# First conditioning part in two halves of output channels, and the last expert pair in a loop of its own

## What is computed

```python
def adaln_layer(x, mod, lp, s0_f, s0_b, ctx_ckv, ctx_krope):
    sh1, sc1, gt1, sh2, sc2, gt2 = jnp.split(mod, 6, axis=-1)
    h = rmsnorm(x, lp['g_norm1']) * (1 + sc1) + sh1
    mix, s_f, s_b, ckv_n, krope = token_mixers(h, lp, s0_f, s0_b, ctx_ckv, ctx_krope)
    x = x + gt1 * mix
    h = rmsnorm(x, lp['g_norm2']) * (1 + sc2) + sh2
    x = x + gt2 * moe(h, lp)
```

## Time and profile before

| | |
|---|---|
| median of three runs | 856.54 us (855.97 to 858.58) |
| the profiled execution's own time | 856.37 us |
| its span | 854.5 us |
| TensorE busy | 809.0 us, 95% |
| VectorE busy | 396.8 us, 46% |
| ScalarE busy | 140.5 us, 16% |
| moved from and to memory | 257.62 MB, mean 301 GB/s |

### The profile page before, as it was taken

The page is one execution under the profiler, slowest core; times in us unless marked ns, Lnnn a source line. Parts: engine busy times, 40 slices in busy tenths (PEclk is TensorE's granted clock), DMA queues, the critical chain, the costliest instruction groups (busy, mean ns, idle before and its releaser), DMA issues.

```text
span 854.5 us, 14663 instructions
## 1 busy us (share of the span) xinstructions
PE 809.0 (95%) x5589; PEld 423.0 (49%) x5589; DVE 396.8 (46%) x841; ACT 140.5 (16%) x289; POOL 8.3 (1%) x16
## 2 busy tenths in 40 slices
PE   3699999879999999999999999999999999999993
PEld 0355434556545645535545455355454554553552
DVE  1206485573787434443443344334434433443346
ACT  2122110210232201111111111111111111111110
POOL 0000001000000000000000000000000000000000
PEclk9799999989999999999999999999999999999998
DMA  9975445424402999989989989899899899898905
GB/s 352 396 289 185 177 147 197 197 74 163 182 26 69 424 368 366 402 349 387 381 350 395 376 345 419 349 375 392 354 384 379 350 402 371 344 420 352 375 0 196
DMA packets 41780, 257.62 MB, mean 301 GB/s; under 512 B 4572, under 2 KB 7004, under 8 KB 13472
## 3 DMA queue, kind: packets, MB, share of 16 engines
q1 hardware_dynamic: 41760, 257.35, 75.8%
HBM read 253.81 MB, written 3.52 MB: 301 GB/s over the span
## 4 chain that ended last, share of the span: by engine, by line
PE 87%; DVE 7%; DMA 3%; ACT 1%; issue 1%; SPq 0%; DVEq 0%; ACTq 0%
PE ps L508 85%; DMA ada<-in_w_ada 3%; PE ps L948 1%; DVE h L1529 0%; DVE h L1530 0%; DVE x1b L1764 0%; DVE acc L1763 0%; ACT sq L1112 0%; DVE probT L1436 0%; PE ps L783 0%; DVE x L1519 0%; DVE xtmp L1517 0%; DVE attn L1425 0%; DVE keyT L1403 0%; SPq L381 0%
## 5 line engine op out<-in xcount | busy, mean ns | idle before, releaser
L508 PE MATMUL ps<-raw_gu,xs 128*32 128x512 f32 x2048 | 225.6, 592 | 0.0
L508 PEld LDWEIGHTS ps<-raw_gu,xs 128*32 128x32 f32 x2048 | 66.5, 110 | 152.6 <-issue 152.6
L1733 DVE TENSOR_TENSOR acc<-acc,ps 128x512 f32<-128x512 f32 x198 | 120.9, 679 | 0.8 <-PE ps L508 0.8
L508 PE MATMUL ps<-raw_dn,ast 128*32 128x512 f32 x1024 | 116.5, 595 | 0.0
L508 PE MATMUL ps<-ys,place 128*128 128x512 f32 x396 | 107.9, 409 | 1.4 <-DVE ys L1726 1.4
L508 PE MATMUL ps<-pick,h2h 128*128 128x256 f32 x408 | 98.6, 283 | 0.9 <-issue 0.9
L508 PE MATMUL ps<-pick,h2l 128*128 128x256 f32 x408 | 98.6, 283 | 0.0
L1718 DVE SCALAR_TENSOR_TENSOR act_a<-ps,small,sil 128x256 f32<-128x256 f32 x32 | 15.5, 484 | 176.9 <-ACT sil L1174 176.9
L508 PEld LDWEIGHTS ps<-ys,place 128*128 128x128 f32 x396 | 69.6, 189 | 41.1 <-issue 26.8
L508 PEld LDWEIGHTS ps<-pick,h2h 128*128 128x128 f32 x408 | 78.2, 192 | 2.3 <-issue 1.7
L508 PEld LDWEIGHTS ps<-pick,h2l 128*128 128x128 f32 x408 | 78.2, 192 | 0.6
(11 more groups left out here) (283 smaller groups left out, 632.7 us busy)
## 6 DMA issues: line engine op xcount, KB each, us to landing
raw_gu<-in_w_exp_gate SPq DMA_DIRECT2D x64, 1024.0 KB, 8.5
raw_gu<-in_w_exp_up SPq DMA_DIRECT2D x64, 1024.0 KB, 10.8
raw_dn<-in_w_exp_down SPq DMA_DIRECT2D x64, 1024.0 KB, 8.1
ada<-in_w_ada SPq DMA_DIRECT2D x8, 1024.0 KB, 10.2
ada2a<-in_w_ada SPq DMA_DIRECT2D x8, 1024.0 KB, 4.6
ada2b<-in_w_ada SPq DMA_DIRECT2D x8, 1024.0 KB, 4.7
w_out<-in_w_out SPq DMA_DIRECT2D x1, 4096.0 KB, 13.0
w_qk<-in_w_in SPq DMA_DIRECT2D x1, 2048.0 KB, 19.6
```

The costliest lines, as they stand in the source:

```text
L508: return nc.tensor.matmul(out, l, r, start=first, stop=last)
L1733: V.tensor_tensor(a, a, ps[:, 4 + (6 * half + k) % 4, :], ALU.add).then_inc(S["acc_done"], 1)
```

## The change

The first third of `w_ada` is fetched in two passes of eight transfers of 512 KB, pass h with the output columns h * 512 to h * 512 + 511 of shift and of scale (two runs of 2 KB per partition). Each chunk has its own buffer; the second pass of chunk c waits for the first pass's products of that chunk. `hT`'s chunks are now rows c * 128 + p of the model width, so that the first half of the output columns completes chunks 0 to 3; `w_in` is read in that order, and `w_mla` and `w_qk` in two halves by chunk. TensorE runs the first pass, turns it, turns `x_sb`, and puts the second pass's products between the first halves of the `mla` products. The constants `tconst`, `rows` and `wgk` are issued later. In the expert part the last pair has its own loop on TensorE, ScalarE and VectorE, without gather, gate columns, `tokens` and `picks`; the number of pairs before it is a second number in `jobs`.

The diff, cut to its core:

```diff
@@ -377,22 +377,27 @@
-            for c in range(4):
-                sp.dma_start(ada1[:, c, :], w_ada[:, c, 0:2 * D]).then_inc(ada1_in[c], 16)
+            w_in = A["w_in"][0].rearrange("(c p) n -> p c n", p=P)
+            low, high = slice(0, NC // 2), slice(NC // 2, NC)
+            for h in range(2):
+                for c in range(NC):
+                    if h:
+                        sp.wait_ge(S["ada1_used"], c + 1)
+                    cols_ = w_ada[:, c, 0:2 * D].rearrange("p (j n) -> p j n", j=2)[:, :, h * 512:(h + 1) * 512]
+                    sp.dma_start(ada1[:, c], cols_).then_inc(ada1_in[c], 16)
+                if not h:
+                    load(w_mla[:, low], w_in[:, low, 1536:1984], "w_mla_in")
+            load(w_qk[:, low], w_in[:, low, 0:512], "w_qk_in")
+            load(w_mla[:, high], w_in[:, high, 1536:1984], "w_mla2_in")
+            load(w_qk[:, high], w_in[:, high, 0:512], "w_qk2_in")
             load(tconst[:], A["c_trunk"], "consts_in")
             load(rows[:], A["c_rows"].partition_broadcast(P), "consts_in")
             load(wgk[:], A["c_wgk"], "consts_in")
-            w_in = rows_pc(A["w_in"][0], 1984)
-            for c in range(4, NC):
-                sp.wait_ge(S["ada1_used"], c - 3)
-                sp.dma_start(ada1[:, c - 4, :], w_ada[:, c, 0:2 * D]).then_inc(ada1_in[c - 4], 16)
-            load(w_mla[:], w_in[:, :, 1536:1984], "w_mla_in")
-            load(w_qk[:], w_in[:, :, 0:512], "w_qk_in")
             load(krope[:, 3, :], A["cache_mla_krope"][0, 0], "cache_in")
             load(ckvn[:, 3, :], A["cache_mla_ckv"][0, 0], "cache_in")
             load(w_v[:], w_in[:, :, 512:1024], "w_v_in")
             load(w_g[:], w_in[:, :, 1024:1536], "w_g_in")
-            sp.wait_ge(S["ada1_used"], NC)
+            sp.wait_ge(S["ada1_used"], 2 * NC)
@@ -539,58 +544,83 @@
-            for c in range(NC):
-                if c == 4:
-                    pe.wait_ge(S["consts_in"], 16)
-                    pe.wait_ge(S["xn_ready"], 1)
-                    for k in range(NC):
-                        if k >= 4:
-                            pe.wait_ge(S["xT_sb"], k - 3)
-                        for t in range(NT):
-                            last = nc.tensor.transpose(ps[:, 4 + k % 4, t * P:(t + 1) * P],
-                                                       x_sb[:, t, k::NC], ident)
-                        last.then_inc(S["xT_done"], 1)
-                pe.wait_ge(ada1_in[c % 4], 16 * (c // 4 + 1))
-                for n in range(4):
-                    last = mm(ps[32 * n:32 * n + 2, 0, :], silu_c[:, c, :], ada1[:, c % 4, n * 512:(n + 1) * 512], c == 0, c == NC - 1)
+
+            def ada1_piece(h, c):
+                pe.wait_ge(ada1_in[c], 16 * (h + 1))
+                for j in range(2):
+                    for q in range(2):
+                        r = 32 * (2 * j + q)
+                        last = mm(ps[r:r + 2, 4 * h, 0:256], silu_c[:, c, :], ada1[:, c, j, q * 256:(q + 1) * 256], c == 0, c == NC - 1)
                 last.then_inc(S["ada1_used"], 1)
...
+            def mod_t(h):
+                pe.wait_ge(S["mod1_sb"], h + 1)
+                if h:
+                    pe.wait_ge(S["xT_sb"], NC)
+                for k in range(4):
+                    rows_ = ident[0:98, 32 * (k // 2):32 * (k // 2) + 66].rearrange("p (j s) -> p j s", s=2)[:, 0::32, :]
+                    last = mm(ps[:, 5, 16 * h + 4 * k:16 * h + 4 * k + 4], mod1[0:98, h, k % 2 * P:(k % 2 + 1) * P], rows_, True, True)
+                last.then_inc(S["modT_done"], 1)
+
+            def token_rows(n, t, w, cs=range(NC)):
+                o = (open_proj(n) if cs[0] == 0 else pbank(n))[:, 0:w.shape[2]]
+                for c in cs:
                     if n == "mla0":
                         pe.wait_ge(S["h_ready"], c + 1)
...
-                last.then_inc(S["proj_done"], 1)
...
+                if cs[-1] == NC - 1:
+                    last.then_inc(S["proj_done"], 1)
...
+            def qk_rows(k, cs=range(NC)):
+                if cs[0] == 0 and k:
+                    pe.wait_ge(S["lr_sb"], NT)
+                o = (open_proj(f"qk{k}") if cs[0] == 0 else pbank(f"qk{k}"))[:, 0:TOK]
...
+
+            for c in range(NC):
+                ada1_piece(0, c)
+            pe.wait_ge(S["consts_in"], 16)
+            mod_t(0)
+            pe.wait_ge(S["xn_ready"], 1)
+            for k in range(NC):
+                if k == 1:
+                    pe.wait_ge(S["mod_cols"], 1)
+                if k >= 4:
+                    pe.wait_ge(S["xT_sb"], k - 3)
+                for t in range(NT):
+                    last = nc.tensor.transpose(ps[:, 4 + k % 4, t * P:(t + 1) * P], x_sb[:, t, k * P:(k + 1) * P], ident)
+                last.then_inc(S["xT_done"], 1)
+            pe.wait_ge(S["w_mla_in"], 16)
+            first, second = range(NC // 2), range(NC // 2, NC)
+            pe.wait_ge(S["mod1_sb"], 1)
+            token_rows("mla0", 0, w_mla, first)
+            pe.wait_ge(S["xT_sb"], 5)
+            for c in range(3):
+                ada1_piece(1, c)
+            token_rows("mla1", 1, w_mla, first)
+            for c in range(3, 6):
+                ada1_piece(1, c)
+            token_rows("mla2", 2, w_mla, first)
+            for c in range(6, NC):
+                ada1_piece(1, c)
+            mod_t(1)
             pe.wait_ge(S["w_qk_in"], 16)
+            qk_rows(0, first)
+            pe.wait_ge(S["w_mla2_in"], 16)
+            for t in range(NT):
+                token_rows(f"mla{t}", t, w_mla, second)
+            pe.wait_ge(S["w_qk2_in"], 16)
             for k in range(4):
-                if k:
-                    pe.wait_ge(S["lr_sb"], NT)
...
+                qk_rows(k, second if k == 0 else range(NC))
...
@@ -962,11 +992,14 @@
                 i = 2 * p + half
+                end = p is n_pairs
...
                     if half or k > 3:
                         pe.wait_ge(S["acc_done"], 6 * i + k - 3)
+                    elif end:
+                        pe.wait_ge(S["acc_done"], 12 * final + 9 + k)
...
@@ -988,8 +1021,9 @@
-            def pair(p, wide):
+            final = pe.value_load(jobs[0:1, NJOB + 1:NJOB + 2], min_val=NMAIN // 2 - 1, max_val=NUNIT // 2 - 1)
+
+            def pair(p, wide, more=True):
...
@@ -999,18 +1033,21 @@
-                pe.wait_ge(S["pick_ready"], p + 2)
-                for q in range(4):
-                    pe.wait_ge(S["acc_done"], 12 * p + 9 + q)
-                    gather(p + 1, q)
-                pe.wait_ge(S["ast_ready"], 2 * p + 3)
-                gate_slots(2 * p + 2)
+                if more:
+                    pe.wait_ge(S["pick_ready"], p + 2)
+                    for q in range(4):
+                        pe.wait_ge(S["acc_done"], 12 * p + 9 + q)
+                        gather(p + 1, q)
+                    pe.wait_ge(S["ast_ready"], 2 * p + 3)
+                    gate_slots(2 * p + 2)
                 down(p, 1, wide)
 
             with pe.Fori(0, WIDE // 2) as p:
                 pair(p, True)
-            with pe.Fori(WIDE // 2, n_pairs) as p:
+            with pe.Fori(WIDE // 2, final) as p:
                 pair(p, False)
+            with pe.Fori(final, n_pairs) as p:
+                pair(p, False, False)
@@ -1198,16 +1235,24 @@
-            with act.Fori(0, n_pairs) as p:
+            final = act.value_load(jobs[0:1, NJOB + 1:NJOB + 2], min_val=NMAIN // 2 - 1, max_val=NUNIT // 2 - 1)
+
+            def pair(p, more):
...
+                if more:
+                    act.wait_ge(S["up_done"], 2 * p + 2)
+                    tokens(p + 1, 0)
+                    tokens(p + 1, 2)
                 high_y(p, 1)
+
+            with act.Fori(0, final) as p:
+                pair(p, True)
+            with act.Fori(final, n_pairs) as p:
+                pair(p, False)
 
@@ -1263,22 +1309,25 @@
-            dve.wait_ge(S["ada1_used"], NC)
-            V.tensor_copy(mod1[0:98], ps[0:98, 0, :]).then_inc(S["mod1_sb"], 1)
-            dve.wait_ge(S["modT_done"], 1)
...
-            V.memset(ps[:, 4, :], 0.0).then_inc(S["bank4_zero"], 1)
...
-            dve.wait_ge(S["xT_sb"], NC)
...
+            for h in range(2):
+                dve.wait_ge(S["ada1_used"], NC * (h + 1))
+                V.tensor_copy(mod1[0:98, h], ps[0:98, 4 * h, 0:256]).then_inc(S["mod1_sb"], 1)
+                dve.wait_ge(S["modT_done"], h + 1)
+                a, b = 4 * h, 4 * h + 4
...
+                dve.sem_inc(S["mod_cols"], 1)
+                for c in range(a, b):
+                    dve.wait_ge(S["xT_sb"], c + 1)
+                    for s, x, y in ((0, 0, P), (1, P, TOK)):
+                        last = V.tensor_scalar(hT[:, c, x:y], hT[:, c, x:y], scale1[:, c, s:s + 1], modc[:, c, s:s + 1],
+                                               ALU.mult, ALU.add)
+                    last.then_inc(S["h_ready"], 1)
@@ -1741,21 +1791,30 @@
-            with dve.Fori(0, n_pairs) as p:
-                dve.wait_ge(S["gates_done"], p + 1)
```

(78 more changed lines are left out.)

32 lines of the change are left out of this document (7 added, 25 removed).

## The result

The changed kernel takes 846.67 us in the median of four runs (844.67 to 847.11); the kernel before, 856.68. The ratio is 0.9875, 95% interval 0.9853 to 0.9898: 10.0 us or 1.25% faster. The forecast was 848.3, range 844.3 to 851.5. The profiled execution took 846.39 us, with a span of 844.6.

A forecast was written before the change was run, and what follows sets the result against it. TensorE, with 87% of the chain that ended last, was taken to bound the kernel. The terms -4.0 + 2.2 - 6.3 = -8.1 us against the profiled 856.37 gave 848.3, range 844.3 to 851.5.

The forecast's parts named there:

- Step 1, TensorE's queue: At the start: with work moved ahead, TensorE reaches `ada2a` at 53.7; by its queue alone 6 to 10 us gained.
- Step 2, the wait: At the first `ada2a` products: TensorE idles until `ada2a` lands at 59.4 instead of starting at 63.4, gaining 4.0 us.
- The price of 2 KB rows: At the start: 8 MB moving in 2 KB rows instead of 8 KB rows makes `ada2a` land 1.8 us later.
- the rest of SyncE's queue: Transfers behind SyncE's later wait for `ada1` products, which ends at 39 to 42, are still issued early enough: no cost.
- Step 3, the clock: Behind the idle time before `ada2a`: half clock for 3.4 to 5.6 us, costing 2.2 us (1.7 to 2.8).
- clock kept: Rival at `ada2a`: TensorE arrives at 57, idles 2.3 us and the clock stays up, giving 846.1 us; chance 18%.
- main case: Whole kernel: landing gains 4.0 us, clock costs 2.2, last pair gains 6.3, giving 848.3 us; chance 48%.
- Second part: Last expert pair, half 1: 48 gather and 6 gate products go, so down products start sooner, gaining 6.3 us.
- The switch: Expert part: changing to the last pair's own loop on each engine costs 0 us.
- its 1.2 us: Last pair: VectorE's additions end at 829.71, its first `low_y` is due at 830.9, so 1.2 us are to spare.

The follow-up runs named there:

- e8: The changed kernel again, unedited, on the chip of some later runs: 845.89 us, ratio 0.9874 to the kernel before.
- e4: The kernel before with every 1024 KB `ada1` transfer issued as two of 512 KB in 2 KB rows: 858.33 us, ratio 1.003.
- e5: The changed kernel with one more transfer of 1024 KB into free memory ahead of the first `ada2a`: 849.98 us, ratio 0.9924 to the kernel before.
- e6: The changed kernel with two more transfers, 1792 KB, into free memory ahead of the first `ada2a`: 852.52 us, ratio 0.9962 to the kernel before.
- e2: The kernel before with only the last pair's own loops added, its old start kept: 849.89 us, ratio 0.9922.
- e3: The changed kernel with the first four `ada2a` products moved behind the second `w_qk` block: 844.36 us, ratio 0.985 to the kernel before.
- e9: The changed kernel with `x_sb` transposed between the first pass's last products and first `ada2a` products behind the second `w_qk` block: 842.19 us, ratio 0.985 to the kernel before.
- e1: The kernel before with only the two-pass start, its old expert loops kept: 852.38 us, ratio 0.9957.

## Why the prediction was right

**Step 1, TensorE's queue: right in kind, 4 us too early.** The forecast had TensorE at `ada2a` at 53.7, and 55.4 to 57.1 with the clock at half for a while; it came at 57.7 (58.8 in e8). The first pass ended where it should (20.1 + 1.0 for 21.1). The missing part lies between 21 and 28: eight turned instructions took 1.84 us, not 0.5, since I scaled by their number, and one with 128 weight columns took 0.23 us where one with 64 had taken 0.065 (2.09 over 32), both at 1.2 GHz; and the transposes took 4.78 us at TensorE's own pace, not at ScalarE's 0.40 per chunk. Why the wider one costs 3.5 times as much was not tried. From 28.07 it needed 29.6 us to 57.66, where 28.7 were counted. The slow start was allowed for in the upper end only, as an addition to the projection, and not in the steps ahead of it.

**Step 2, the wait: right.** `ada2a` landed at 59.74 for 59.4; the gain is 3.6 us for 4.0. The price of 2 KB rows, the least certain term (1.8), is borne out by itself in e4: 2.74 us per 1024 KB at the end, as taken from another tensor's rows, and 1.4 to 1.6 us over the eight chunks. The Trainium skill's figure in "DMA: Bandwidth & Descriptors", section "Specifications" (full rate from 512 B), would have put the landing at 57.6 and e4 at no difference; here 2 KB rows are slower than 8 KB rows, so the measurement decides against it. That the rest of SyncE's queue would not suffer held: `ada2a` was issued at 48.15, 11.6 us before landing, as before (11.7).

**Step 3, the clock: the step that failed**, 2.2 us forecast, 0 measured. The rival "clock kept" (18%) is what happened, by the path that it names: a late arrival, an idle time of 2.1 us. It was given too little because the arrival was put at 53.7. So the main case (48%), whose own range was 846.8 to 850, is not what happened: the measured 846.67 lies just below it, and the profile's 846.39 beside the rival's 846.1. The stated range held because it was made to hold this rival too. e5 and e6 show the term at 2.35 and 2.5 us once the idle time is 5.3 and 5.8.

**Second part: right.** 6.3 forecast, 6.33 in the trace (9.97 - 3.64), 6.1 in e2. The switch cost nothing, VectorE had its 1.2 us.

**Sum.** The profile has -3.6 - 6.3 = -9.9; the forecast -8.1. The whole difference of 1.8 is the clock's 2.2 less the 0.4 by which the landing was later.

## What to carry to other kernels

When work is moved ahead of a transfer that used to arrive early, find out how long that transfer lay waiting: this distance, and not the work moved, is the most that can be gained. Behind it, the product that waits can often change places with one that doesn't, as e3 does with a two-line edit. A median and a trace of one execution are not to be added up: here a stretch that the change does not touch moves the time by 1.6 us from one execution to the next. A price that hangs on an idle time (the clock's) must be worked out from the arrival's range and not from its earliest value.

## What was not expected of the hardware

- The clock can fall without any idle time. In e3 and in e8 TensorE was busy without a gap, with products of two weight columns (`ada2a`, `ada2b`), products over 32 rows of the contraction (`lrT`) and then transposes, and fell to 1.2 GHz, near 67 and 70 us, 10 us or more behind its last idle time. e3's stretches:

```profile
64.00:66.00 2.00, 2.00 (x7) 1.18 (x7) 1.18 (x2) 0.00 (x0) 0.00 (x0) 1.00 1.01 295
66.00:68.00 2.00, 2.00 (x12) 1.46 (x11) 1.87 (x4) 0.66 (x1) 0.00 (x0) 0.75 1.00 422
68.00:70.00 2.00, 2.00 (x11) 0.33 (x10) 1.25 (x4) 1.97 (x2) 0.00 (x0) 0.50 0.80 332
```

  In the other nine profiles, the kernel before, the changed one and e9 among them, the same transposes ran at 2.4 GHz. Why it falls in one run and not in another was not tried.
- The granted clock reads 1.00 in all of the first 25 us, though a piece of 256 columns takes 1.03 us there and 0.61 later (e9): the column is to be believed only from its first change on, and before that the durations tell the level.
- A dense start brings the clock up some microseconds earlier (e9), and 1.44 us of waiting right behind it was followed by the lower level again. In the changed kernel 2.12 us, in the middle of a long busy stretch, was not. So the idle time alone does not tell whether the clock falls.
- The first products of the output projection, behind an idle time of 3.63 to 3.65 us in every profile, took between 8.53 and 10.10 us, as the clock came back sooner or later. e1 and e8:

```profile
182.02 8.58 PE L513 MATMUL ps<-w_out,mixedT 128*128 128x512 f32 x16 [3.64 <-DVE mixedT L1498]
183.36 10.10 PE L513 MATMUL ps<-w_out,mixedT 128*128 128x512 f32 x16 [3.63 <-DVE mixedT L1513]
```

  The kernel before has 9.91 and the changed one 9.83, so their difference is free of it; e3 has 10.05, e5 8.53, e6 8.62 and e9 8.80.
